# A transformer-and-RWKV kernel on one core: the remainder of each rounded weight tile is subtracted by VectorE instead of GpSimd

## The reference, cut to what matters

```
for i in 0, 1:                                  # first block, 528 tokens
    h = rmsnorm(hres, g[i,0])
    m = diff_attention(h) if i == 0 else short_conv(h)   # w_in 1024x3072, w_out 1024x1024
    hres = hres + rmsnorm(m, g[i,1])
    h = rmsnorm(hres, g[i,2])
    hres = hres + rmsnorm(relu(h @ w_up)**2 @ w_down, g[i,3])   # 1024x4096, 4096x1024
x = hres[:, 16:]
z = rmsnorm(x) @ w_in_2                          # second block, 512 tokens, 1024x3200
y_a = pooling over windows 2, 4, 8, 16, mixed by small matrices
y_b = rwkv7_time_mix(token-shifted z)            # a scan, done in chunks of 64 tokens
y = concat(y_a * silu(gate_a), y_b * silu(gate_b))
out = rmsnorm(x + y @ w_out_2, final_gain)
```

## Time and profile before

| | |
|---|---|
| median of three runs | 1791.09 us |
| span of the profiled execution, first to last instruction | 1788.9 us |
| around the span, against the median run | 2.2 us |
| TensorE busy | 1691.3 us, 95% |
| VectorE busy | 776.1 us, 43% |
| ScalarE busy | 633.6 us, 35% |
| GpSimd busy | 622.9 us, 35% |
| mean granted TensorE clock | 0.966 of 2.4 GHz |

### The profile page before, as it was taken

The page is one execution under the profiler, slowest core; times in us unless marked ns, Lnnn a source line. Parts: engine busy times, 40 slices in busy tenths (PEclk is TensorE's granted clock), DMA queues, the critical chain, the costliest instruction groups (busy, mean ns, idle before and its releaser), DMA issues.

```text
span 1788.9 us, 30446 instructions
## 1 busy us (share of the span) xinstructions
PE 1691.3 (95%) x12096; PEld 1486.3 (83%) x12096; DVE 776.1 (43%) x1263; ACT 633.6 (35%) x1163; POOL 622.9 (35%) x315
## 2 busy tenths in 40 slices
PE   7999998889999999899998999999998999999995
PEld 7788886889999999889977788888877777888764
DVE  3333332374323231554527441414148986444436
ACT  5555654253222232322224432323235343322222
POOL 2222220354444443444435444444444445300011
PEclk9999996899999999999999999999999999988898
DMA  5111110213332233222321223323321222000001
GB/s 191 48 48 48 48 48 12 71 60 95 95 94 88 91 95 95 72 65 89 94 83 47 95 95 94 95 95 97 96 78 60 83 83 83 3 2 1 2 24 47
DMA packets 35397, 125.59 MB, mean 70 GB/s; under 512 B 3920, under 2 KB 4048, under 8 KB 35280
## 3 DMA queue, kind: packets, MB, share of 16 engines
q1 hardware_dynamic: 35280, 123.90, 22.4%
HBM read 121.79 MB, written 2.10 MB: 69 GB/s over the span
## 4 chain that ended last, share of the span: by engine, by line
PE 82%; DVE 11%; issue 3%; ACT 2%; POOL 2%; DMA 0%; DVEq 0%; SPq 0%; POOLq 0%; ACTq 0%
PE G L1346 62%; PE G L1583 5%; PE ST L1583 3%; PE PV L1583 3%; PE PV L1460 2%; DVE t L910 2%; PE PO L1583 1%; DVE rstd L845 1%; POOL wlo L445 1%; DVE xl L851 1%; PE ST L1319 1%; PE ST L1435 1%; PE G L1435 1%; PE G L1433 1%; PE PO L1449 1%
## 5 line engine op out<-in xcount | busy, mean ns | idle before, releaser
L445 POOL TENSOR_TENSOR wlo<-raw,whi 128x1024 fp32r<-128x1024 f32 x225 | 547.3, 2433 | 1106.8 <-ACT whi L505 745.9
L1346 PE MATMUL G<-xh,whi 128*128 128x256 f32 (+3 forms) x1552 | 386.4, 313 | 4.5 <-POOL wlo L445 2.7
L1346 PE MATMUL G<-xl,whi 128*128 128x256 f32 (+3 forms) x1552 | 368.7, 301 | 0.0
L1346 PE MATMUL G<-xh,wlo 128*128 128x256 f32 (+3 forms) x1552 | 366.7, 300 | 0.0
L1346 PE MATMUL G<-ah,whi 128*128 128x258 f32 (+2 forms) x992 | 271.4, 321 | 10.1 <-POOL wlo L445 5.6
L1346 PEld LDWEIGHTS G<-xh,whi 128*128 128x128 f32 x1552 | 251.5, 190 | 30.6 <-issue 11.8
L516 ACT ACTIVATE whi<-raw 128x1024 fp32r<-128x1024 f32 x112 | 118.8, 1060 | 429.6 <-PE G L1346 429.6
L1346 PE MATMUL G<-al,whi 128*128 128x258 f32 (+2 forms) x992 | 268.6, 318 | 0.0
L1346 PE MATMUL G<-ah,wlo 128*128 128x258 f32 (+2 forms) x992 | 268.1, 318 | 0.0
L1346 PEld LDWEIGHTS G<-xl,whi 128*128 128x128 f32 x1552 | 250.9, 189 | 12.2
L1346 PEld LDWEIGHTS G<-xh,wlo 128*128 128x128 f32 x1552 | 251.9, 189 | 10.2
(11 more groups left out here) (284 smaller groups left out, 2130.7 us busy)
## 6 DMA issues: line engine op xcount, KB each, us to landing
raw<-weights_dram SPq DMA_DIRECT2D x225, 512.0 KB, 3.6
hres<-xT_dram SPq DMA_DIRECT2D x8, 264.0 KB, 6.4
out_dram<-hres SPq DMA_DIRECT2D x8, 256.0 KB, 2.1
con<-consts_dram SPq DMA_DIRECT2D x1, 512.0 KB, 9.3
mat<-mats_dram SPq DMA_DIRECT2D x1, 512.0 KB, 10.1
con<-consts_dram SPq DMA_DIRECT2D x1, 392.0 KB, 5.9
vec<-vecs_dram SPq DMA_DIRECT2D x1, 203.0 KB, 2.5
```

The lines of the kernel that those rows point to most:

```text
L445: nc.gpsimd.tensor_tensor(wlo[:, s % 2], raw[:, s], whi[:, s % 2].bitcast(F32), ALU.subtract)\
L1346: last_of[0] = nc.tensor.matmul(to[:, p0:p1], wt[:, w, ws], xt[:, k, t0 - off:t1_ - off], start=k == 0 and q == 0, stop=k == KT - 1 and q ...
```

## The change: what it does, and the diff

GpSimd loses all 225 subtractions `low`. What stays with it is `residual` in the four transitions and the pooling of the second block (lines 478 to 490). VectorE gets them: a function `low(b, s)` with the same instruction, the same two waits and the same semaphore, called behind the eviction of each block for the block two further on. In the transitions, in the prologue, in `ENDS` and in the last loop single calls are placed by hand. All other instructions keep their order.

```diff
         @block.gpsimd
-            def low(b, j, s):
-                pool.wait_ge(hi_ready, b + 1)
-                if not isinstance(b, int) or b >= 2:
-                    pool.wait_ge(block_done, b - 1)
-                nc.gpsimd.tensor_tensor(wlo[:, s % 2], raw[:, s], whi[:, s % 2].bitcast(F32), ALU.subtract)\
-                    .then_inc(lo_ready, 1)
...
-            done = 0
-            for i, (b, cols) in enumerate(((B_MLP[0], NEED), (B_CI, NEED), (B_MLP[1], OUT), (B_IN2, OUT))):
-                blocks(pool, done, b + 1 - done, low)
+            for i, cols in enumerate((NEED, NEED, OUT, OUT)):
                 residual(i, 0, cols)
-                low(b + 1, 1, (b + 1) % 4)
                 residual(i, 1, cols)
-                done = b + 2
-            blocks(pool, done, B_O2 + 2 - done, low)
...
-            blocks(pool, B_O2 + 2, KT - 2, low)
...
         @block.vector
+            def low(b, s):
+                if isinstance(b, int) and b >= NBLK:
+                    return
+                dve.wait_ge(hi_ready, b + 1)
+                if not isinstance(b, int) or b >= 2:
+                    dve.wait_ge(block_done, b - 1)
+                nc.vector.tensor_tensor(wlo[:, s % 2], raw[:, s], whi[:, s % 2].bitcast(F32), ALU.subtract)\
+                    .then_inc(lo_ready, 1)
...
             def out_tiles(b0, cols, before):        # MLP down blocks
                     tile_to_m(j, G[s % 2], slice(0, cols[1] - cols[0]), block_slice(cols), before, tile_out)
+                    low(b + 2, (s + 2) % 4)
...
             def last_tiles(i, b0, cols, before, norm, pre):     # transitions
                     tile_to_m(j, G[j % 2], slice(0, cols[1] - cols[0]), block_slice(cols), before, tile_out)
+                    low(b0 + j + 2, (b0 + j + 2) % 4)
                     if j >= 1:
                         add_square(i, j - 1, cols)
...
                         elif k == 0 and half == 0:
                             half_tile(KT - 2, 1)
+                            low(b0 + KT, (b0 + KT) % 4)
                         elif k == 1 and half == 0:
                             add_square(i, KT - 2, cols, 1)
                             half_tile(KT - 1, 1)
+                        if k == 3 and half == 0:
+                            low(b0 + KT + 1, (b0 + KT + 1) % 4)
...
-                            low(j, s4)              # MLP up blocks
+                            low_a(j, s4)
+                            low(b + 2, (s4 + 2) % 4)
...
+            low(0, 0)                               # prologue
             for k in range(KT):
                 low_x(0, 0, 0, k, ALL)
+                if k == 5:
+                    low(1, 1)
...
                     dve.wait_ge(block_done, s + 1)  # turns of attention
                     nc.vector.scalar_tensor_tensor((qT, kT, vT)[r][:, h % 2, :], qkv_acc(s)[:, pos], 0.125 if r == 0 else 1.0,
                                                    rstd[:, 0, :], ALU.mult, ALU.mult).then_inc(tile_out, 1)
+                    low(s + 2, (s + 2) % 4)
                 for t in cur[1:]:
                     differences(t)
...
                     elif kind == out_:              # ENDS
                         if n + 2 < KT - 1:
                             last_low(n + 2)
+                        if n % KT == KT - 1:
+                            b = B_O2 + n // KT + 2
+                            low(b, b % 4)
...
             for j in range(KT):
+                if j == 3:
+                    low(NBLK - 1, (NBLK - 1) % 4)
```

More of the change, by code:

```diff
@@ L933, in mlp, with low_a @@
                         n0 = 32 * layer + 8 * c
-                        def low(j, s4):
+                        def low_a(j, s4):
                             dve.wait_ge(a_hi, j + (8 * f + 1))
@@ L1061, in _ @@
                         .then_inc(tile_out, 1)
+                    low(b + 2, (b + 2) % 4)
                 dve.wait_ge(tile_out, B_CI + 3 * j + 3)
```

## The result

The changed kernel took 1808.97 us (median of four runs, 1805.42 to 1812.53) against 1789.38 us for the kernel before in the same comparison (four runs, 1786.61 to 1791.23). The ratio is 1.0111, with a 95% interval of 1.0092 to 1.013: slower by 1.1%. The profiled executions differ by as much, 1807.4 us after and 1788.9 us before. The forecast was 1809 us.

The account below looks back on a forecast made before the run. TensorE, busy 1691.3 of 1788.9 us, bounds the kernel, so only places where it waits count. The terms sum to +18.1 us: 1807.0 us profiled, 1809 us as a run (+1.0%), range 1797 to 1820 us.

Parts of the forecast that it names:

- attention's queue: In attention, the subtraction on VectorE delays `differences` and `head_low`, for which TensorE's scores wait: 16.6 us, bounds 8 to 24.
- The price of a subtraction: On VectorE, one subtraction of 1024 elements was estimated at 1.26 us, bounds 1.1 to 1.4.
- Steady MLP: In steady MLP blocks `wlo` is ready at about 4.1 of 5.7 us, hidden by TensorE's next block: cost 0.
- k turns: End of a k block's turn in attention: `head_low` and the ST scores come 1.7 us later, six times, 10.3 us.
- What the profile would show: For attention's k turns: a new TensorE wait of about 1.7 us before the ST scores, put down to `al`.
- q turns: End of a q block's turn in attention: `negs` and TensorE's second scores come 0.9 us later, seven times, 6.3 us.
- The clock rival: In attention, each of six 1.7 us stalls brings a half-clock stretch, 12 us on top: 1821 us; chance 11%.
- MLP starts: At both MLP starts VectorE subtracts `wlo` only after `al`, so TensorE resumes 2.3 us later each, 4.6 us.
- Transitions: In four transitions `wlo` ends earlier and `t` and `xl` escape GpSimd: -1.8 us each, -7.4 us, bounds -11 and -2.
- RWKV start: At the start of the RWKV steps, block 218's subtraction delays memsets and masks TensorE waits for: +1.8 us, bounds 1 to 3.
- ENDS: In the final scan and group norm, subtractions of blocks 219 to 221 and 223 delay VectorE's chain: +4.5 us.
- the start and IN2: Part of the rest, with the first attention output block: relief from GpSimd's blocking, -2 us, bounds -6 and 0.

Follow-up runs that it names:

- k-turns-only kernel: The changed kernel with attention's subtraction right behind the eviction only in k blocks' turns, elsewhere behind the next turn's `negs`: 1795.99 us, ratio 1.0046 to the kernel before.
- kernel with all moved late: The changed kernel with attention's subtractions still on VectorE, but moved from behind the eviction to behind the next turn's `negs`: 1786.98 us, ratio 0.999 to the kernel before.

## Why the prediction was right

The result, 1808.97 us, is the forecast's 1809, and its mechanism, attention's queue, is shown by three kernels: the loss goes and comes with attention's subtractions, and goes when only their place changes. That the sum was met so closely is luck, since its errors cancel.

- **The price of a subtraction**: 1.238 us against 1.26.
- **Steady MLP, 0**: right.
- **k turns, 1.7 x 6 = 10.3**: 1.54 each, 9.2 in all; the k-turns-only kernel took 9.0 us more. Right in size and place. What the profile would show was half wrong: not a wait of 1.7 us but one of 0.35 and two products that no longer overlap.
- **q turns, 0.9 x 7 = 6.3**: the term that was mis-sized. In an ordinary head the wait is 0.57 us longer: the scores came 3.00 us behind the eviction's start (176.88) before and 3.57 after. VectorE starts the subtraction 1.15 us behind the eviction's start where GpSimd took 1.27, it holds the queue 1.15 us and not 1.2, and `differences` takes 0.73 and not 0.82. But the first head waits 1.7 us longer, since it has no slack ahead of `negs`. That makes 6 x 0.57 + 1.7 = 5.1 us of waiting, and behind these waits the clock falls. The q turns measured 15 us alone.
- **The clock rival** (11%) was a mechanism that acts beside the forecast and not in place of it, at 1.3 to 1.5 us an event in an ordinary head, and with the place wrong: it belongs to the q turn's wait and not to the k turn's. Its "Attention now runs at full clock" holds for the heads up to 271 us; from there to 323 us the profile before has four falls, 37 us at the lower level. The Trainium skill, "TensorE: Matmul & The Clock Gate", section "HAM oscillation — how this bites in real kernels", describes a loop in which every wait for a DMA, of some 3 to 5 us, costs the clock. Such waits are longer than the rival's 1.7 us, so the section does not carry the rival's sum. The traces agree with it in part: the clock fell behind waits of 1.24 us too, but in three heads of five (0.69, 0.72, 0.76), and with no k turn of these heads (1.00).
- **MLP starts, 2.3 each**: 2.25 and 2.6 us with the clock held up, 4.7 and 4.1 as it ran. The wait was right, the clock behind it was missing.
- **Transitions, -7.4**: -13.7 measured. By shape, `t` at the transitions (64 of them) went from 53.2 to 44.2 us of VectorE's time and `xl` (48) from 29.8 to 25.0, so the direction is right. In blocks 96 to 98 and 120 to 130 the profile before has 5 us of lost clock (0.90 and 0.89 in two stretches of 8 us, then 0.86, 0.93, 0.85 and 0.94), and the one after none. Other kernels here with the same instructions in blocks 120 to 130 gained 1.8 to 4.4 us there, so these falls come and go without a change there. With the 5 us out, -8.6 is left.
- **RWKV start +1.8, ENDS +4.5**: 0.9 and 5.6. The steps 219 to 220 and 220 to 221 cost 0.5 each (0.75 said). The step from 221 to 222 took 1.9 us more, but that is not the subtraction's price: the kernel with only attention's subtractions moved has there the instructions of before and took 3.1 us more. Its granted clock there was 0.76, 0.81 and 0.62 in the three stretches of 4 us from 1744.5, where the kernel before had 1.00. In the changed kernel the clock fell there too (0.61 from 1755 to 1759). At the RWKV start the kernel with only attention's subtractions moved took 0.6 us more with no change there. So of the 6.5 us from block 210 on some 4 are the change's (estimate: 6.5 less 1.9 and 0.6), where the two terms said 6.3. The way from the first reciprocal to TensorE's first product took 9.09 us before and 11.37 after, +2.3 as worked out:

```profile
1763.22 0.95 DVE L1264 RECIPROCAL acc<-rms 128x128 f32<-128x128 f32 x1 [1.28 <-ACT rms L792]
1767.13 1.22 DVE L836 TENSOR_TENSOR wlo<-raw,whi 128x1024 fp32r<-128x1024 f32 x1 [2.96 <-ACT whi L492]
1768.28 2.57 DVE L1264 RECIPROCAL acc<-rms 128x128 f32<-128x128 f32 x3
...
1774.59 0.80 PE L1597 MATMUL G<-x2h,whi 128*128 128x512 f32 x1 [7.26 <-DVE x2l L1282]
```

Taken together: attention is 21.9 us above the kernel with all moved late (+20.6 against -1.3), of which the measured queue terms are 9.2 + 6 x 0.57 + 1.7 = 14.3; the other 7.6, and some 4 at the MLP starts, go with the clock. That is some 12 us beyond the queue arithmetic. Against it stand 6 us more than forecast in the transitions, of which 5 are the clock of the profile before, 2.3 us in attention, whose queue terms came to 14.3 and not 16.6, 1.3 us by which attention was faster than before apart from them, and 1.8 us in the start and IN2 (-3.8 against -2).

## What to carry to other kernels

An engine that is 43% busy can take some 280 us of work more and the kernel gains 0.9%, or loses 1.1%: what decides is what stands behind the new instruction in the engine's queue, and whether TensorE waits for it. Replay the queue at each such place, put the instruction behind what TensorE waits for, and where it can't be moved, cut it: half of it behind the wait was worth 11 of 15 us here. Price a new or longer TensorE wait with what the clock does behind it: in attention that was 7.6 us beside 14.3 of queue, at the MLP starts 4 beside 4.9, and in the q turns alone more than the waits. Before reading a difference of 1 to 3 us in one stage of one profile, compare kernels whose instructions there are the same.

## What was not expected of the hardware

- The granted clock fell to the 1.2 GHz level behind waits of TensorE of 3.1 us (and stayed there over 5 us behind it), of 2.75 and 2.2 us, in three of five like cases behind 1.24 to 1.52 us, and in the first head in some profiles behind 1.08 us. In attention's seven q turns it never fell behind 0.7 us, nor in heads 2 to 6 in the k turns, where 1.5 us was lost but TensorE was kept busy with half of its rows. Which of the like cases it takes differs between kernels with the same instructions there.
- Two products of 64 rows that run side by side take 1.2 us for 2 x 2 matmuls of 512 columns, one behind the other 1.1 us each. The 1.6 us that a late `al` costs shows as 0.35 us of waiting; the rest is the lost overlap and reads as busy.
- VectorE's subtraction of 128x1024 takes 1.24 us where GpSimd's took 2.37, and an `al` of 128x512 that ran beside GpSimd's took 1805 ns against 693 alone. Moving the work took about 160 us off VectorE's other instructions, of which TensorE got back some 11 us at most (8.6 in the transitions and 2.2 in IN2).
